# A projection stage on one core: straight code, with the next tile's norm and turn inside the tile at work

## The chip, the cores and the metric

The kernel runs on one core of one Trainium2 chip. The metric is the time of one execution on the device, in microseconds. The kernel before took 4375.03 us (median of three runs, 4374.49 to 4392.1). A profile gives one execution in detail; its times are microseconds from the first instruction.

## The reference, cut to what matters

One layer of a hybrid model in float32, for 1024 prompt rows and 8 sequences of 8 sample rows, 1024 wide. What the change touches is the first half of the layer: the norm, the projection by `w_in`, the short convolution and the mLSTM with its running state.

```
mod = silu(c) @ w_ada + b_ada                       # six rows of shift, scale and gate
h = rmsnorm(x, norm1_g) * (1 + scale1) + shift1
aq, ak, av, mqk, mv, mo, mi, mf = split(h @ w_in)   # w_in: 1024 x 3592
aq, ak = rmsnorm per head                           # k and v rows are outputs too
qk = silu(conv4(mqk)); lf = log_sigmoid(mf + b)
per chunk: b = cumsum(lf); mt = max(b + m, max(D)); wD = exp(D - mt)
           num = wg * (q @ C) + (q @ k.T * wD) @ v; den likewise with n
           hA = num / max(|den|, exp(-mt)); C, n, m = updated
hA = rmsnorm(hA) * sigmoid(mo)
att = dilated attention of aq, ak, av               # second half, not touched
x = x + gate1 * (concat(hA, att) @ w_out); x = x + gate2 * peer(...)
```

## The kernel before, in words

The program has three stages with a barrier between them. `stage0` makes the modulation rows and bias tables. `stage1`, the projection stage, makes q, k, v and the mLSTM's output. `stage3` does the attention, the output projection and the retrieval of experts, and takes most of the time; the change does not touch it.

`stage1` goes through nine tiles in order: eight of 128 prompt rows (kind "p") and one of the 64 sample rows (kind "s"). Each engine has its own list of instructions for a tile, and the lists meet by semaphores (`sig[...]`). The first tile is written out, tiles 1 to 7 are a hardware loop on each engine (`Fori`), and the sample tile is written out again. There is one buffer for x, one for the normed rows `h`, one for the turned rows `h_t`.

Within a tile the order is: ScalarE squares and sums the rows of x (L490) and makes the inverse rms (L485, L486, shared with the heads' norm); VectorE norms the rows (L665, L666); TensorE turns them by eight transposes into PSUM banks 0 and 1 (L564), and ScalarE copies them into `h_t` (L496). TensorE then multiplies `h_t` by parts of `w_in`: the gates, 8 columns wide (L569); mqk, 128 matmuls with 128 (sample tile 64) moving columns (L572); mv, mo, the two halves of qk, and av, each sixteen matmuls of 512 columns (`project`, L556). Between them stand small matmuls of the mLSTM: the cumulative sums (L579, L580), diag_a (L585), diag_m, diag_d and the selection (L588 to L590), the scores (L598), the turn of k (L601, "ktok"), the output (L613, L614), and the update of the state (L619, "cup").

VectorE's list is: gates (L668), lf (L670), the copy of mqk to `ext` and the convolution (L675 to L695), the small rows and diag_a (L698 to L702), the running maximum, diag_m and diag_d (L707 to L714), arg (L720), og (L723 to L725), scores, q_carry and kws (L729 to L742), the q and k norm (L745 to L753, ends with `qk_n`), the raw hidden rows (L759 to L765, `hraw`), their norm (L770, L771), and the state (L775 to L779). ScalarE's list is: rms, turned rows, log-sigmoid (L500 to L502), copies and exponentials of what TensorE leaves in PSUM, Silu of the convolution (L513), decay (L518), carry (L521), the squares of q and k (L528) and their inverse rms, av's copy (L534), the hidden rows' rms.

SyncE loads x for a tile as soon as the tile before has been normed (L408), then the sample rows' modulation, and after the eighth tile's state the sample's state and convolution tails (L434). GpSimd stores q, k, v and the hidden rows of each tile (L449 to L456) and, once, zeros (L462). ScalarE's queue also issues copies of the caches, 16 x 4 MB, before its first tile (L477).

Of the kernel before, what the change touches and what calls it, by code (L numbers as in the profile page):

```python
# [196 lines left out]
PER_P, PER_S = 59, 59  # L197
# [137 lines left out]
def stage1(nc, block, sig, mem, psum, const, ins, outs, scratch):  # L335
# [32 lines left out]
    s_state = work.take(DB, H_A, DK + 1)  # L368
# [36 lines left out]
    def _(sp):  # L405
# [8 lines left out]
        with sp.Fori(1, NT) as i:  # L414
            tile(i, P, ins["x"][bass.ds(i * P, P), :])
# [29 lines left out]
    def _(pool):  # L445
# [17 lines left out]
        with pool.Fori(1, NT) as i:  # L463
            store(i, P, bass.ds(i * P, P), bass.ds(i * P + WBUF - SEQ, P))
# [6 lines left out]
    def _(act):  # L471
# [8 lines left out]
        def tile(i, rows, kind, per):  # L480
            chain = Chain(act, sig["act1"], i * per)
# [6 lines left out]
            act.wait_ge(sig["x_in"], (i + 1) * 16)  # L488
            act.wait_ge(sig["h"], i)
            chain.link(nc.scalar.activation(squares[0:rows], x[0:rows], ACT.Square, accum_out=xss[0:rows]))  # L490
            inv_rms(xrs[0:rows], xln[0:rows], xss[0:rows], D, "x_rms")
            act.wait_ge(sig["h_t_ps"], i + 1)
            act.wait_ge(sig["av_ps"], i)
            for half in range(2):
                src = psum[:, half].rearrange("p (k t) -> p k t", k=4)[:, :, 0:rows]
                cp = nc.scalar.activation(h_t[:, 4 * half:4 * half + 4, 0:rows], src, ACT.Copy)  # L496
                cp.then_inc(sig["h_t"], 1)

# [3 lines left out]
            nc.scalar.activation(sm["soft"][0:rows], sm["soft"][0:rows], ACT.Ln, bias=1.0).then_inc(sig["soft"], 1)  # L502

# [9 lines left out]
            nc.scalar.activation(conv[:, :, 0:rows], conv_y[:, :, 0:rows], ACT.Silu).then_inc(sig["silu"], 1)  # L513

# [28 lines left out]
            assert chain.n == per, chain.n  # L543

        tile(0, P, "p", 7)
        with act.Fori(1, NT) as i:
            tile(i, P, "p", 7)
        tile(NT, NS, "s", 7)

    @block.tensor  # L550
    def _(pe):
        ident, ones = const["ident"], const["ones"]

        def project(bank, col, n, rows, at=0):
            for k in range(KD):
                mm = nc.tensor.matmul(psum[0:rows, bank, at:at + n], h_t[:, k, 0:rows], w_in[:, k, col:col + n], start=k == 0, stop=k == KD - 1)  # L556
            return mm

        def tile(i, rows, kind):
# [5 lines left out]
            tr.then_inc(sig["h_t_ps"], 1)  # L565
            pe.wait_ge(sig["h_t"], 2 * i + 2)
            pe.wait_ge(sig["w_in_in"], 16 * KD)
            pe.wait_ge(sig["mnew"], i)
            project(7, O_G, 2 * H_A, rows).then_inc(sig["gates_ps"], 1)  # L569
            for c in range(8):  # L570
                for k in range(KD):
                    mm = nc.tensor.matmul(psum[:, c // 4, c % 4 * P:c % 4 * P + rows], w_in[:, k, O_QK + c * P:O_QK + (c + 1) * P],  # L572
                                          h_t[:, k, 0:rows], start=k == 0, stop=k == KD - 1)
# [25 lines left out]
            mm.then_inc(sig["s_ps"], 1)  # L599
            for hh in range(H_A):  # L600
# [3 lines left out]
            project(4, 2 * W_B, W_B, rows).then_inc(sig["av_ps"], 1)  # L604
# [17 lines left out]
        tile(0, P, "p")  # L622
        with pe.Fori(1, NT) as i:
# [26 lines left out]
    def _(dve):  # L650
# [4 lines left out]
        def tile(i, rows, kind, per):  # L655
            chain = Chain(dve, sig["dve1"], dve_base + i * per)
# [6 lines left out]
            dve.wait_ge(sig["x_rms"], i + 1)  # L663
            dve.wait_ge(sig["h_t_ps"], i)
            chain.link(v.scalar_tensor_tensor(out=h[R], in0=x[R], scalar=xrs[R], in1=mod[R, 1], op0=ALU.mult, op1=ALU.mult))  # L665
            v.tensor_tensor(h[R], h[R], mod[R, 0], ALU.add).then_inc(sig["h"], 1)  # L666
# [3 lines left out]
            v.scalar_tensor_tensor(out=s("lf"), in0=gates[R, H_A:], scalar=0.0, in1=s("soft"), op0=ALU.min, op1=ALU.subtract).then_inc(sig["lf"], 1)  # L670

            dve.wait_ge(sig["mqk_ps"], i + 1)
            dve.wait_ge(sig["silu"], i)
            if kind == "p":
                chain.link(v.tensor_copy(ext_p[:, :, HALO:], psum[:, 0:2].rearrange("p a (c t) -> p (a c) t", c=4)))  # L675
# [988 lines left out]
```

## Time and profile before

| | |
|---|---|
| time, median of three runs | 4375.03 us |
| profiled execution | 4374.66 us, span 4373.0 us |
| TensorE busy over the span | 3560.7 us (81%) |
| VectorE, ScalarE, GpSimd | 2393.2, 1640.2, 1279.2 us |
| `stage1`, from the first turn to the state's store | 212.3 to 1005.4 us |
| `stage3`, from its first load | 1013.5 us to the end |

Windows give the busy time of each engine between two times, with the clock that TensorE was granted as a share of 2.4 GHz. In a timeline each row is a run of equal instructions: start, time covered, engine, line, operation, and in brackets how long the engine was idle before and which instruction ended the wait. "mem" is the on-chip memory and "psum" the accumulator banks. "PE" is TensorE, "PEld" its weight loads, "DVE" VectorE, "ACT" ScalarE, "POOL" GpSimd, "SP" SyncE. A float32 matmul is two instructions, so counts are twice those of the source.

### The profile page before, as it was taken

What the parts mean: (1) busy time and instruction counts of PE and PEld (TensorE: products, weight loads), DVE (VectorE), ACT (ScalarE), POOL (GpSimd) and SP (SyncE); (2) the same over time, 40 slices, a digit from 0 to 9 for tenths busy, and PEclk for the clock granted to TensorE, in tenths of its full rate; (3) what the DMA queues carried; (4) which work ended last, traced back from release to release, by engine and by line L of the source; (5) the groups of instructions that cost most, each with busy time, mean ns of one, the idle gap of its engine ahead of it and who ended that gap; (6) DMA issues with size and microseconds to landing.
All of it is one profiled execution on the core that took longest, in us unless ns stands there. A gap on an engine that the chain in (4) does not pass through costs nothing.

```text
span 4373.0 us, 38660 instructions
## 1 busy us (share of the span) xinstructions
PE 3560.7 (81%) x12228; PEld 1818.6 (42%) x12228; DVE 2393.2 (55%) x5587; ACT 1640.2 (38%) x4396; POOL 1279.2 (29%) x1204
## 2 busy tenths in 40 slices
PE   7288788684867987997898898789799888989877
PEld 1054454453533533443453444445345344524321
DVE  1033433322464784595486468449646845947844
ACT  0022322311335335435434533543453354334333
POOL 0000000000223343343343334234334434435433
PEclk9688888865989999999999899999999999999999
DMA  6897100146669999999999899999999999999998
GB/s 237 301 338 252 38 19 19 43 23 262 237 236 372 400 415 358 403 411 391 372 414 416 329 394 413 360 387 410 413 376 390 410 394 395 397 374 401 411 408 368
DMA packets 251979, 1419.95 MB, mean 325 GB/s; under 512 B 42963, under 2 KB 65875, under 8 KB 105603
## 3 DMA queue, kind: packets, MB, share of 16 engines
q0 software_dynamic: 168768, 1200.70, 68.4%
q1 hardware_dynamic: 79588, 132.71, 9.8%
q10 hardware_dynamic: 3440, 84.35, 5.5%
q8 instruction: 84, 1.38, 0.1%
q14 instruction: 99, 0.81, 0.1%
HBM read 1385.48 MB, written 98.73 MB: 339 GB/s over the span
## 4 chain that ended last, share of the span: by engine, by line
PE 30%; DMA 24%; DVE 11%; ACT 8%; issue 2%; POOL 0%; SPq 0%; ACTq 0%; POOLq 0%; DVEq 0%
DMA mem<-in_experts,mem 21%; PE psum L1279 20%; DVE mem L1573 6%; PE psum L1196 3%; PE psum L1178 3%; DMA mem<-key_cols 2%; ACT L1383 2%; DVE mem L1439 1%; ACT mem L1387 1%; DVE mem L1438 1%; ACT mem L1384 1%; ACT L1306 1%; PE psum L1134 1%; ACT mem L1306 1%; ACT mem L1383 1%
## 5 line engine op out<-in xcount | busy, mean ns | idle before, releaser
L1279 PE MATMUL psum<-mem 128*128 128x512 f32 (+1 forms) x4352 | 2141.1, 626 | 387.9 <-ACT mem L1387 386.4
L1104 POOL DMA_INDIRECT mem<-in_experts,mem x1088 | 1213.3, 1115 | 1872.9 <-PE psum L1279 1804.2
L1573 DVE CUSTOM_DVE_ANT_0 mem<-mem 128x1024 f32<-128x1024 f32 x1088 | 1322.8, 1222 | 708.5 <-DMA mem<-in_experts,mem 695.7
L1279 PEld LDWEIGHTS psum<-mem 128*128 128x128 f32 (+1 forms) x4352 | 776.8, 193 | 1471.1 <-ACT mem L1387 747.7
L1383 ACT ACTIVATE mem<-mem 128x1 f32<-128x1 f32 x1088 | 219.2, 201 | 1562.9 <-DVE mem L1573 1560.2
L1387 ACT ACTIVATE mem<-mem 128x128 f32<-128x128 f32 (+1 forms) x1088 | 433.3, 398 | 35.6
L556 PE MATMUL psum<-mem 128*128 128x512 f32 (+3 forms) x864 | 351.2, 558 | 10.2 <-ACT mem L496 10.2
L1384 ACT ACTIVATE mem<-mem 128x1 f32<-128x1 f32 x1088 | 320.4, 295 | 35.3
L1196 PEld LDWEIGHTS psum<-mem 128*128 128x128 f32 x2304 | 274.4, 191 | 45.2 <-issue 41.8
L1196 PE MATMUL psum<-mem 128*128 128x128 f32 (+1 forms) x2304 | 282.1, 276 | 2.5 <-ACT mem L1335 2.5
L556 PEld LDWEIGHTS psum<-mem 128*128 128x128 f32 (+1 forms) x864 | 159.7, 207 | 176.7 <-issue 162.9
L449 POOL DMA_DIRECT2D qkv_rows<-mem x9 | 5.1, 563 | 742.1 <-ACT mem L534 742.1
L564 PE MATMUL psum<-mem 128*128 128x128 f32 (+1 forms) x72 | 16.9, 415 | 192.0 <-DVE mem L666 192.0
L572 PE MATMUL psum<-mem 128*128 128x128 f32 (+1 forms) x1152 | 158.9, 310 | 0.0
L572 PEld LDWEIGHTS psum<-mem 128*128 128x128 f32 x1152 | 157.8, 226 | 0.0
L1416 DVE CUSTOM_DVE_ANT_0 mem<-psum,mem 128x128 f32<-128x128 f32 (+7 forms) x64 | 48.4, 756 | 192.7 <-PE psum L1136 166.0
L1438 DVE MAX8 mem<-mem 128x8 f32<-128x128 f32 (+3 forms) x432 | 145.8, 338 | 12.5
L1439 DVE FIND_INDEX8 mem<-mem 128x8 uint32<-128x128 f32 (+3 forms) x432 | 141.9, 328 | 0.0
L1178 PE MATMUL psum<-mem 128*128 128x512 f32 (+1 forms) x288 | 135.5, 595 | 0.0
L1134 PE MATMUL psum<-mem 64*128 64x512 f32 (+3 forms) x160 | 67.9, 531 | 56.3 <-DMA mem<-key_cols 56.2
L303 PE MATMUL psum<-mem 128*9 128x512 f32 x192 | 91.7, 637 | 20.0 <-DMA mem<-in_b_ada 13.9
L1383 ACT ACT_TABLE_LOAD x80 | 102.6, 1283 | 14.0 <-DVE mem L1573 12.6
(255 smaller groups left out, 2612.4 us busy)
## 6 DMA issues: line engine op xcount, KB each, us to landing
out_k_s<-in_cache_k ACTq DMA_DIRECT2D x8, 4080.0 KB, 125.1
out_v_s<-in_cache_v ACTq DMA_DIRECT2D x8, 4080.0 KB, 137.4
mem<-in_w_ada SPq DMA_DIRECT2D x12, 2048.0 KB
mem<-mod_rows SPq DMA_DIRECT2D x34, 512.0 KB
mem<-in_experts,mem POOLq DMA_INDIRECT x1088, 9.7
mem<-in_keys_t POOLq DMA_DIRECT2D x16, 1024.0 KB, 6.8
mem<-in_vals POOLq DMA_DIRECT2D x16, 1024.0 KB, 8.4
mem<-in_w_in ACTq DMA_DIRECT2D x8, 1796.0 KB, 24.8
```

What stands on the lines that cost most here:

```text
L556: mm = nc.tensor.matmul(psum[0:rows, bank, at:at + n], h_t[:, k, 0:rows], w_in[:, k, col:col + n], start=k == 0, stop=k == KD - 1)
L572: mm = nc.tensor.matmul(psum[:, c // 4, c % 4 * P:c % 4 * P + rows], w_in[:, k, O_QK + c * P:O_QK + (c + 1) * P], h_t[:, k, 0:rows], start ...
L1104: pool.indirect_dma_start(out=ring[:, g % N_SLOTS].rearrange("p a n -> p (a n)"), out_offset=None, in_=ins["experts"][:, :], in_offset=bas ...
L1178: mm = nc.tensor.matmul(psum[0:r, out_banks(n)[half]], turned[:, k, 0:r], w_out[:, k, half * 512:(half + 1) * 512], start=k == 0, stop=k = ...
L1196: mm = nc.tensor.matmul(psum[:, 5, j % 4 * P:j % 4 * P + r], w_q[:, k, j * NKEY:(j + 1) * NKEY], turned[:, k, 0:r], start=k == 0, stop=k = ...
L1279: mm = nc.tensor.matmul(psum[0:r, half], diag[:, g % 4, 0:r], ring[:, g % N_SLOTS, 1, half * 512:(half + 1) * 512], start=c == 0, stop=c = ...
L1383: chain.link(a.activation(act_v[:, c:c + 1], dots[:, c:c + 1], ACT.Gelu))
L1384: chain.link(a.activation(weight[:, c:c + 1], act_v[:, c:c + 1], ACT.Copy, scale=gate[i % 2][:, c:c + 1]))
L1387: a.activation(diag[:, g % 4, 0:r], spread, ACT.Copy, scale=weight[:, c:c + 1]).then_inc(sig["diag"], 1)
L1438: chain.link(v.max(values[:, e:e + 8], src))
L1439: chain.step(v.max_index(places[:, e:e + 8], values[:, e:e + 8], src))
L1573: v.tensor_tensor_reduce(row, row, h2[i % 2], 1.0, 0.0, ALU.mult, ALU.add, dots[:, c:c + 1]).then_inc(sig["dots"], 1)
```

## The change

- The hardware loops on all engines become straight code, so that waits compare with constants.
- The norm and turn of a tile become functions (`rows_rms`, `turned` on ScalarE, `turn` on TensorE, `normed` on VectorE). They are called for tile 0 ahead of the tiles, and for tile i + 1 inside tile i: the rms after the log-sigmoid, the norm after lf, the turn after mo, the copies after Silu.
- A second buffer for the turned rows lies in the room of the sample rows' state, which is loaded after the eighth tile; tiles take turns (`h_ts[i % 2]`).
- On TensorE mv moves ahead of mqk, the first half of qk ahead of diag_a's matmul, the second half between diag_a's and diag_m's. The wait for `hraw` and `kws` of the tile before stands ahead of mqk, that for arg ahead of ktok. diag_a's matmul goes to bank 4, diag_m's to bank 1.
- On VectorE the small rows and diag_a move ahead of the convolution.
- The sample tile's wait for the convolution tails stays at the head of its tile, which now begins with the gates.

The diff, cut: what is moved unchanged is not shown again, nor the loops of SyncE and GpSimd, which change in the same way, nor the bank numbers on VectorE.

```diff
@@ -365,7 +364,9 @@
-    s_state = work.take(DB, H_A, DK + 1)
+    s_room = work.take(DB * H_A * (DK + 1))
+    s_state = s_room.rearrange("p (b h e) -> p b h e", b=DB, h=H_A)
+    h_ts = (h_t, s_room[:, 0:KD * P].rearrange("p (k t) -> p k t", k=KD))
@@ -477,29 +478,40 @@
+        def rows_rms(i, rows):
+            act.wait_ge(sig["x_in"], (i + 1) * 16)
+            act.wait_ge(sig["h"], i)
+            if i >= 2:
+                act.wait_ge(sig["qss"], i - 1)
...
+        def turned(i, rows):
+            act.wait_ge(sig["h_t_ps"], i + 1)
+            if i >= 2:
+                act.wait_ge(sig["av_ps"], i - 1)
...
             nc.scalar.activation(sm["soft"][0:rows], sm["soft"][0:rows], ACT.Ln, bias=1.0).then_inc(sig["soft"], 1)
+            if i < NT:
+                rows_rms(i + 1, P if i + 1 < NT else NS)
...
             nc.scalar.activation(conv[:, :, 0:rows], conv_y[:, :, 0:rows], ACT.Silu).then_inc(sig["silu"], 1)
+            if i < NT:
+                turned(i + 1, P if i + 1 < NT else NS)
@@ -540,68 +554,83 @@
-        tile(0, P, "p", 7)
-        with act.Fori(1, NT) as i:
-            tile(i, P, "p", 7)
-        tile(NT, NS, "s", 7)
+        rows_rms(0, P)
+        turned(0, P)
+        for i in range(NT):
+            tile(i, P, "p")
+        tile(NT, NS, "s")
...
+        def turn(i, rows):
             pe.wait_ge(sig["h"], i + 1)
-            pe.wait_ge(sig["hraw"], i)
-            pe.wait_ge(sig["kws"], i)
+            if i >= 1:
+                pe.wait_ge(sig["ext"], i)
...
+        def tile(i, rows, kind):
             pe.wait_ge(sig["h_t"], 2 * i + 2)
...
+            project(i, 7, O_G, 2 * H_A, rows).then_inc(sig["gates_ps"], 1)
+            if i >= 1:
+                pe.wait_ge(sig["scores"], i)
+            project(i, 5, O_MV, W_A, rows).then_inc(sig["mv_ps"], 1)
+            if i >= 1:
+                pe.wait_ge(sig["hraw"], i)
+                pe.wait_ge(sig["kws"], i)
...
-            pe.wait_ge(sig["scores"], i)
-            project(5, O_MV, W_A, rows).then_inc(sig["mv_ps"], 1)
...
-            project(6, O_MO, W_A, rows).then_inc(sig["mo_ps"], 1)
+            project(i, 6, O_MO, W_A, rows).then_inc(sig["mo_ps"], 1)
+            if i < NT:
+                turn(i + 1, P if i + 1 < NT else NS)
+            if i >= 1:
+                pe.wait_ge(sig["state"], i)
+            project(i, 2, 0, W_B, rows)
 
             pe.wait_ge(sig["diag_a"], i + 1)
-            pe.wait_ge(sig["state"], i)
-            nc.tensor.matmul(psum[0:rows, 2, 0:H_A * rows], ones[0:rows, 0:rows], diag_a_of(rows), start=True, stop=True).then_inc(sig["a_rep"], 1)
+            if i >= 1:
+                pe.wait_ge(sig["av"], i)
+            nc.tensor.matmul(psum[0:rows, 4, 0:H_A * rows], ones[0:rows, 0:rows], diag_a_of(rows), start=True, stop=True).then_inc(sig["a_rep"], 1)
+            project(i, 3, W_B, W_B, rows).then_inc(sig["qk_ps"], 1)
             pe.wait_ge(sig["diag_m"], i + 1)
-            pe.wait_ge(sig["av"], i)
-            nc.tensor.matmul(psum[0:rows, 3, 0:H_A * rows], ones[0:rows, 0:rows], diag_m_of(rows), start=True, stop=True)
+            if i < NT:
+                pe.wait_ge(sig["h_t"], 2 * i + 4)
+            nc.tensor.matmul(psum[0:rows, 1, 0:H_A * rows], ones[0:rows, 0:rows], diag_m_of(rows), start=True, stop=True)
...
-            project(2, 0, W_B, rows)
-            pe.wait_ge(sig["arg"], i + 1)
-            project(3, W_B, W_B, rows).then_inc(sig["qk_ps"], 1)
             pe.wait_ge(sig["silu"], i + 1)
...
             mm.then_inc(sig["s_ps"], 1)
+            pe.wait_ge(sig["arg"], i + 1)
...
             pe.wait_ge(sig["carry"], i + 1)
-            project(4, 2 * W_B, W_B, rows).then_inc(sig["av_ps"], 1)
+            project(i, 4, 2 * W_B, W_B, rows).then_inc(sig["av_ps"], 1)
@@ -652,31 +681,48 @@
+        def normed(i, rows):
+            R = slice(0, rows)
+            dve.wait_ge(sig["x_rms"], i + 1)
+            if i >= 1:
+                dve.wait_ge(sig["h_t_ps"], i)
...
             v.scalar_tensor_tensor(out=s("lf"), in0=gates[R, H_A:], scalar=0.0, in1=s("soft"), op0=ALU.min, op1=ALU.subtract).then_inc(sig["lf"], 1)
+            if i + 1 < NT:
+                normed(i + 1, P)
+            if i + 1 == NT:
+                dve.wait_ge(sig["mod_in"], 64)
+                normed(NT, NS)
...
+                v.tensor_copy(ext_p[:, :, HALO:], psum[:, 0:2].rearrange("p a (c t) -> p (a c) t", c=4)).then_inc(sig["ext"], 1)
+                dve.wait_ge(sig["ext"], i + 1)
...
+            dve.wait_ge(sig["b_ps"], i + 1)
+            chain.step(v.tensor_copy(s("b"), psum[R, 7, 8:12]))
...
@@ -777,22 +816,19 @@
-        tile(0, P, "p", PER_P)
-        with dve.Fori(1, NT) as i:
-            tile(i, P, "p", PER_P)
-        dve.wait_ge(sig["mod_in"], 64)
+        normed(0, P)
+        for i in range(NT):
+            tile(i, P, "p")
         dve.wait_ge(sig["s_conv_in"], 16 * 8)
...
+        tile(NT, NS, "s")
```

## Rows read from the trace of the kernel before

**Rows 1.** Windows by tile: start:end, length, busy by engine, TensorE clock, DMA share

```profile
294.39:376.54 82.15, 65.28 (x280) 42.78 (x280) 32.47 (x76) 24.21 (x43) 2.16 (x4) 0.85 1.01 344
...
458.44:540.30 81.86, 65.21 (x280) 42.69 (x280) 32.47 (x76) 24.21 (x43) 2.15 (x4) 0.85 0.07 26
212.29:294.39 82.10, 65.50 (x280) 42.86 (x281) 32.45 (x76) 24.20 (x43) 4.72 (x6) 0.85 0.99 333
```

**Rows 2.** Timeline, TensorE, eighth tile: start us, length us, idle before in brackets

```profile
786.10 1.97 PE L564 MATMUL psum<-mem 128*128 128x128 f32 x8 [12.10 <-DVE mem L666]
...
789.25 3.58 PE L556 MATMUL psum<-mem 128*128 128x8 f32 x16 [1.18 <-ACT mem L496]
...
792.68 16.39 PE L572 MATMUL psum<-mem 128*128 128x128 f32 x128
...
827.55 2.07 PE L588 MATMUL psum<-mem 128*128 128x512 f32 x2 [3.42 <-DVE mem L714]
...
831.07 13.98 PE L556 MATMUL psum<-mem 128*128 128x512 f32 x32
...
853.09 0.38 PE L613 MATMUL psum<-mem 128*128 128x129 f32 x2
...
854.87 1.06 PE L619 MATMUL psum<-mem 128*128 128x129 f32 x8
```

**Rows 3.** Timeline, VectorE and ScalarE, eighth tile

```profile
795.06 0.16 DVE L670 SCALAR_TENSOR_TENSOR mem<-mem 128x4 f32<-128x4 f32 x1 [2.03 <-ACT mem L502]
...
831.64 0.69 DVE L720 TENSOR_TENSOR mem<-mem,psum 128x512 f32<-128x512 f32 x1
...
833.55 0.57 ACT L521 ACTIVATE mem<-psum 128x512 f32<-128x512 f32 x1
...
836.09 0.69 DVE L725 TENSOR_TENSOR mem<-mem 128x512 f32<-128x512 f32 x1
...
846.05 0.69 DVE L729 TENSOR_TENSOR mem<-psum,mem 128x512 f32<-128x512 f32 x1 [9.27 <-PE psum L598]
...
852.32 1.23 DVE L753 TENSOR_TENSOR mem<-mem 128x1024 f32<-128x1024 f32 x1
...
863.87 0.42 DVE L779 TENSOR_TENSOR mem<-mem,psum 128x258 f32<-128x258 f32 x1
```

**Rows 4.** Windows with the granted clock: mqk of the fourth tile; sample tile

```profile
467.00:468.90 1.90, 1.90 (x11) 1.90 (x10) 0.50 0.00 0
468.90:471.00 2.10, 2.10 (x21) 2.10 (x21) 1.00 0.00 0
...
935.00:940.00 5.00, 2.69 (x10) 1.00 (x9) 2.78 (x12) 3.67 (x4) 0.00 (x0) 0.99 1.79 4
940.00:945.00 5.00, 5.00 (x9) 1.47 (x8) 4.40 (x4) 1.52 (x7) 0.00 (x0) 0.66 1.03 4
```

**Rows 5.** DMA issues, early tiles: count, KB, us to landing

```profile
mem<-in_x SPq DMA_DIRECT2D x1, 512.0 KB, 27.8
...
out_v_p<-mem POOLq DMA_DIRECT2D x1, 256.0 KB, 55.6
mix_rows<-mem POOLq DMA_DIRECT2D x1, 256.0 KB, 62.7
...
out_v_p<-mem POOLq DMA_DIRECT2D x1, 256.0 KB, 47.2
```

**Rows 6.** Timeline, sample tile

```profile
884.28 1.28 DVE L665 SCALAR_TENSOR_TENSOR mem<-mem 64x1024 f32<-64x1024 f32 x1 [19.98 <-DMA mem<-in_conv_tail]
...
886.87 1.11 PE L564 MATMUL psum<-mem 64*128 64x64 f32 x8 [30.94 <-DVE mem L666]
...
890.54 27.57 PE L572 MATMUL psum<-mem 128*128 128x64 f32 x128
...
937.73 0.64 PE L588 MATMUL psum<-mem 64*64 64x256 f32 x2 [2.31 <-DVE mem L714]
...
963.49 10.43 PE L630 MATMUL psum<-mem 128*128 128x8 f32 x64 [0.68 <-ACT mem L534]
```

More of the change, by code:

```diff
@@ L413, in _ @@
         tile(0, P, ins["x"][0:P, :])
-        with sp.Fori(1, NT) as i:
-            tile(i, P, ins["x"][bass.ds(i * P, P), :])
+        for i in range(1, NT):
+            tile(i, P, ins["x"][i * P:(i + 1) * P, :])
         sp.wait_ge(sig["h"], NT)
@@ L462, in _ @@
             pool.dma_start(outs[name][0:WBUF - SEQ].rearrange("(p r) (a n) -> p (r a) n", p=P, a=2), bc(zeros, 1, 2 * (WBUF - SEQ) // P)).then_inc(sig["zeros_out"], 16)
-        with pool.Fori(1, NT) as i:
-            store(i, P, bass.ds(i * P, P), bass.ds(i * P + WBUF - SEQ, P))
+        for i in range(1, NT):
+            store(i, P, slice(i * P, (i + 1) * P), slice(WBUF - SEQ + i * P, WBUF - SEQ + (i + 1) * P))
         store(NT, NS, slice(SEQ, NTOK))
@@ L478, in _ @@
         lnscale, eps = const["lnscale"], const["eps"]
-        def tile(i, rows, kind, per):
-            chain = Chain(act, sig["act1"], i * per)
+        chain = Chain(act, sig["act1"])
+        def rows_rms(i, rows):
[3 more added lines that the diff above has]
+                act.wait_ge(sig["qss"], i - 1)
+            chain.link(nc.scalar.activation(squares[0:rows], x[0:rows], ACT.Square, accum_out=xss[0:rows]))
+            chain.link(nc.scalar.activation(xln[0:rows], xss[0:rows], ACT.Ln, scale=1.0 / D, bias=eps[0:rows]))
+            nc.scalar.activation(xrs[0:rows], xln[0:rows], ACT.Exp, scale=-0.5).then_inc(sig["x_rms"], 1)
+        def turned(i, rows):
+            act.wait_ge(sig["h_t_ps"], i + 1)
+            if i >= 2:
+                act.wait_ge(sig["av_ps"], i - 1)
+            for half in range(2):
+                src = psum[:, half].rearrange("p (k t) -> p k t", k=4)[:, :, 0:rows]
+                cp = nc.scalar.activation(h_ts[i % 2][:, 4 * half:4 * half + 4, 0:rows], src, ACT.Copy)
+                cp.then_inc(sig["h_t"], 1)
+        def tile(i, rows, kind):
             def inv_rms(out, tmp, total, n, event):
@@ L486, in inv_rms @@
                 nc.scalar.activation(out, tmp, ACT.Exp, scale=-0.5).then_inc(sig[event], 1)
[L488 to L497, printed above, removed]
             act.wait_ge(sig["gates"], i + 1)
@@ L620, in tile @@
                 mm.then_inc(sig["cup"], 1)
-        tile(0, P, "p")
-        with pe.Fori(1, NT) as i:
+        turn(0, P)
+        for i in range(NT):
             tile(i, P, "p")
@@ L653, in _, with tile @@
         taps = const["conv"]
-        def tile(i, rows, kind, per):
-            chain = Chain(dve, sig["dve1"], dve_base + i * per)
+        def normed(i, rows):
[3 more added lines that the diff above has]
+                dve.wait_ge(sig["h_t_ps"], i)
+            chain.link(v.scalar_tensor_tensor(out=h[R], in0=x[R], scalar=xrs[R], in1=mod[R, 1], op0=ALU.mult, op1=ALU.mult))
+            v.tensor_tensor(h[R], h[R], mod[R, 0], ALU.add).then_inc(sig["h"], 1)
+        def tile(i, rows, kind):
             R = slice(0, rows)
@@ L679, in tile @@
                 dve.wait_ge(sig["s_ext"], 8)
+            dve.wait_ge(sig["b_ps"], i + 1)
+            chain.step(v.tensor_copy(s("b"), psum[R, 7, 8:12]))
+            chain.step(v.tensor_copy(s("blast"), psum[R, 7, 12:16]))
+            chain.link(v.tensor_tensor(s("a"), gates[R, 0:H_A], psum[R, 7, 8:12], ALU.subtract))
+            chain.step(v.tensor_scalar(s("a_s"), s("a"), lnscale[R], None, ALU.add))
+            v.tensor_tensor(heads_of(diag_a, rows), bc(ident[R, R], 1, H_A), bc(s("a"), 2, rows), ALU.mult).then_inc(sig["diag_a"], 1)
             for j in range(CONV_W):
@@ L695, in tile @@
                 v.tensor_copy(ext_p[:, :, 0:HALO], ext_p[:, :, P:P + HALO]).then_inc(sig["halo"], 1)
-            dve.wait_ge(sig["b_ps"], i + 1)
-            chain.step(v.tensor_copy(s("b"), psum[R, 7, 8:12]))
-            chain.step(v.tensor_copy(s("blast"), psum[R, 7, 12:16]))
-            chain.link(v.tensor_tensor(s("a"), gates[R, 0:H_A], psum[R, 7, 8:12], ALU.subtract))
-            chain.step(v.tensor_scalar(s("a_s"), s("a"), lnscale[R], None, ALU.add))
-            v.tensor_tensor(heads_of(diag_a, rows), bc(ident[R, R], 1, H_A), bc(s("a"), 2, rows), ALU.mult).then_inc(sig["diag_a"], 1)
             dve.wait_ge(sig["a_rep"], i + 1)
@@ L706, in tile @@
                 dve.wait_ge(sig["s_state_in"], 32)
-            chain.link(v.tensor_tensor(arg_of(rows), heads_ps(2, rows, rows), bc(const[kind + "_neg"][R], 1, H_A), ALU.add))
+            chain.link(v.tensor_tensor(arg_of(rows), heads_ps(4, rows, rows), bc(const[kind + "_neg"][R], 1, H_A), ALU.add))
             chain.link(v.tensor_reduce(s("cmax"), arg_of(rows), AX.X, ALU.max))
@@ L785, in _ @@
         v.memset(sm["mprev"], 0.0).then_inc(sig["dve1"], 1)
[L786 to L787 removed]
+        dve.wait_ge(sig["dve1"], 4)
         dve.wait_ge(sig["mod_in"], 32)
[L789 to L792 removed]
+        chain = Chain(dve, sig["dve1"], 4)
+        normed(0, P)
+        for i in range(NT):
+            tile(i, P, "p")
         dve.wait_ge(sig["s_conv_in"], 16 * 8)
[L794 to L795 removed]
+        tile(NT, NS, "s")
         chain = Chain(dve, sig["s_state_steps"])
```

29 lines of the change are left out of this document (9 added, 20 removed).

## The prediction

> **What bounds the kernel now.** I read the windows first, one for each tile of the projection stage: it is nine tiles long, and a prompt tile takes 81.9 to 82.15 us, in which TensorE is busy for 65.2, VectorE for 32.5 and ScalarE for 24.2 [rows 1]. TensorE is the longest engine, but 16.7 us of every tile it does nothing, so no engine bounds the stage by itself. The timeline of one tile says where [rows 2]: 12.10 us before the eight transposes at L564, which wait for the next tile's norm on VectorE, 1.18 us before the gates' matmuls (ScalarE copies the turned rows out of PSUM), and 3.42 us at L588 (VectorE makes diag_m). The 12.10 us are one chain: TensorE ends at 855.93 with L619 [rows 2], VectorE ends the state at 864.29 [rows 3], ScalarE's rms and VectorE's norm follow. The first two tiles run while old copies fill the DMA engines (DMA share 0.99 and 1.01, against 0.07 later), and take no longer for it [rows 1].
>
> The idle time costs twice. After it TensorE's clock is granted at 0.50 (1.2 GHz) until 468.9 in the tile that starts at 458.44 and at 1.00 (2.4 GHz) from there [rows 1, 4]. Of these 10.46 us, 1.18 are idle, so the work in them would take 4.6 us less at 2.4 GHz. At L588 four 512-column matmuls and a small one take from 827.55 to 831.07, 3.52 us, where sixteen take 6.99 [rows 2]: another 1.6 us. TensorE's work at full clock is thus 65.2 - 4.6 - 1.6 = 59.0 us a tile.
>
> **A steady prompt tile after the change.** Time 0 is the end of the tile before's L619. The next tile's transposes and their copies now stand inside this tile, so its first matmuls wait for nothing: the 12.10 and 1.18 us go. The 3.42 us go too, since a projection of 6.99 us now stands between diag_a's matmul and diag_m's, and VectorE needs 3.4 us in that place. What is late next, engine by engine:
> - VectorE ends the old tile's state at 8.36 (864.29 - 855.93). Then come the gates and lf, 2.5 us (from 792.68, the end of the gates' matmuls, to 795.22) [rows 2, 3], at about 11. TensorE wants lf only after gates, mv (6.99) and mqk (13.8, half of the 27.57 that 128 such pieces take at 1.2 GHz [rows 6]), at 22.5: hidden, 11 us to spare. The moved rms and norm follow; in the old tile both lay in the 12.10 us, so they end by 23, and the ext copy follows mqk at 24; the turn starts at 29.5: hidden. The two copies of the turned rows come after Silu, near 36, and are wanted at 45: hidden.
> - The added wait on arg, ahead of ktok: after the m matmuls VectorE needs until 832.33 for arg, 1.25 us past 831.07 [rows 2, 3]; the scores' matmuls cover 0.9. Stall 0.4.
> - carry was covered by two projections; now only ktok (0.45) stands before the av projection that waits for it, and carry ends 1.8 us after arg (834.12 - 832.33) [rows 3]. Stall 1.35.
> - The last matmuls (L619) wait for qk_n. From arg VectorE needs 4.45 us for og (836.78 - 832.33) and then, from scores to the last qk product, 7.5 us (846.05 to 853.55) [rows 3], in all 11.95. TensorE needs 0.45 + 1.35 + 6.99 + 1.78 (854.87 - 853.09 [rows 2]) = 10.6. Stall 1.35.
>
> The sum is 59.0 + 3.1 = 62.1 us a tile if the clock stays at 2.4 GHz. It will not quite: from the last stall over L619 to the gates' 8-column matmuls lie four sparse microseconds. The trace has no such stretch; the nearest row is the sample tile's, where a wait of 2.31 us among small matmuls was followed by a mean clock of 0.66 over 5 us, a loss of (1 - 0.66) x 5 = 1.7 us [rows 4, 6]. Bounds are 0 (nothing falls) and 5.4: gates at half rate (1.8), then 4 us of projection at half rate (2.0) as in the old tile's start, and the old L588's 1.6 again at carry. I take 1.7, the nearest row: 63.8 us. From the second tile's start (294.39) to the eighth's (786.10) the old tiles took 491.71, 81.95 each [rows 1, 2]; 7 x (81.95 - 63.8) = 127.0 us gained.
>
> On the clock the Trainium skill ("TensorE: Matmul & The Clock Gate", section "HAM oscillation — how this bites in real kernels") puts the fall down to long idle gaps between bursts of matmuls. By that alone stalls of 1.35 us would leave 2.4 GHz and the tile would take 62.1, a rival below; the row with 2.31 us speaks against it.
>
> **The first tiles, under the copies.** ScalarE's and VectorE's queues now hold the next tile's rms and norm in the middle, and behind them the whole conv and mlstm work, so the load of x must have landed. The second tile's x is asked for at 212.4, as the first turn starts [rows 1], and takes 27.8 us [rows 5]: 240.6 with its issue, norm done at 246.3, 4.6 after mqk. TensorE is at mo until 249 then; ext is copied at 247.5 and the turn waits for nothing. The first tile's L619 ends at 280.8 instead of 282.3 (294.39 less a wait of 12.1 [rows 1, 2]): 1.5 gained. Later loads are asked for a whole tile ahead. Had this one taken the 62.7 us of the slowest row [rows 5], 33 us would be lost once.
> Stores come closer. The first tile's v rows were on their way 55.6 us, its mix rows 62.7 [rows 5]; in the second tile qkv is wanted at 341 (landed at 337), and the old hid at 344 (landed at 351): what waits is the hraw chain, whose 7 us TensorE's gates and mv cover. The second tile's v rows, issued near 344, land between 391 (47.2 us [rows 5]) and 411.7, when the old ones did with the same bytes to drain; they are wanted at 404 ahead of qk_n, on the path. 0 to 8 us; I take the middle, 4 lost. SP's loop becomes straight code that waits for the same norms; POOL's stores keep their order.
>
> **The sample tile.** Its norm waited with the rest for the conv tails (19.98 us, TensorE idle for 30.94 [rows 6]). That wait now stands ahead of its gates' add only; norm and turn lie in the eighth tile, and gates, mv and mqk run at once. lf comes 28.35 + 2.5 = 30.85 after L619 (884.28 - 855.93 [rows 6]). mqk starts at 9 and ends at 23 (full clock) to 37 (half: in the old run these 64-column pieces never left 1.2 GHz though TensorE had no pause). I take 34, since mv's wide columns start it fast. From mqk's end to L630 the old run took 45.4 us (918.1 to 963.49 [rows 6]), 9.4 of it mv, which is now ahead: 36.0. L630 starts at 70 instead of 107.56: 37.5 gained, bounds 34.5 and 40.8. All behind it stays, and the third stage does not touch what moves.
>
> **Sum.** 127.0 + 1.5 - 4 + 37.5 = 162.0. The profiled execution took 4374.66 (span 4373.0 and 1.66 around it), 0.4 under the median of 4375.03, so the forecast is 4213 us.
>
> **Rivals.**
> - The clock stays up and the stores are in time: 62.1 a tile, 12 us less, and the 4 back: 4197. For it: no stall above 1.4 us. Against: the 2.31 us row [rows 6].
> - The clock falls in both sparse stretches: bound 5.4 in place of 1.7, 3.7 x 7 = 26 more: 4239. For it: the old tile's slow start.
> - The unrolling itself gains or costs. Straight code (first tile, 82.10), a loop's first pass (82.15) and a later one (81.86) [rows 1] differ by 0.3 us at most, so a back edge is worth 2 us in seven tiles unless the 12.10 us hid it; if it hid a price, that goes with the wait. The other way, new code for each tile must come in while copies fill the DMA engines; at the price of a load there (27.8) in the three tiles under them: 4213 + 83 = 4296. That is also the case in which the change does not do what it says, since the overlap is lost while engines stand.
> - Slower than before: a denser stage does not hold 2.4 GHz. mqk in the sample tile is the row that speaks for it: 27.57 us at 1.2 GHz without a pause [rows 6]. At 1.2 GHz throughout a tile takes 2 x 59.0 + 3.1 = 121.1 us, 39.2 more than 81.95, in all 274 lost against some 36 gained elsewhere: about 4613. It decides from 23 us lost a tile (162 / 7), which is 46 us of each tile spent at half clock. Against it: within the old tile, 128-column matmuls bring the clock up to 1.00 [rows 4], and with the five projections they are 48.8 of the 59.0 us.
>
> **How the numbers follow.** Chances: the forecast 0.45 (4203 to 4225), full clock 0.22, two falls 0.22, code or loads late in the first tiles 0.07, half clock 0.03, no effect 0.01. 0.5% is 22 us, about what a measurement of this kernel tells from no change. Only the last two cases are not faster by that: faster 0.96, same 0.01, slower 0.03. The range takes in both clock cases, the bounds of the sample tile and a few us either way for the third stage: 4183 to 4250.
>
> **What would show it.** Right: about 64 us between two L619 groups, no idle over 2 us on TensorE inside a prompt tile, waits for arg, carry and qk_n of 0.4 to 1.4 us, the clock mostly at 1.00, L630 about 70 us after the eighth L619. Wrong: a wait at the turn for the ext copy or the norm, VectorE reaching qk_n later than 12 us after arg, a tile longer than 68 us, the sample tile's mqk waiting for anything, or a third stage of another length.

## The result and the profile after

The changed kernel takes 4200.59 us (median of four runs, 4191.22 to 4221.66) against 4380.3 us for the kernel before (median of four): a ratio of 0.959 (95% interval 0.955 to 0.964). Forecast were 4213 us and a range of 4183 to 4250. The profiled execution took 4200.74 us, its span 4199.0, 174.0 under the span of before.

Where the 174.0 us came from, read off the starts of the same groups of matmuls in the two timelines of TensorE (a cup's end is taken 1.00 us behind its start, here and in every run below):

| part | before | after | difference | forecast |
|---|---|---|---|---|
| start to the first turn | 212.29 | 203.89 | -8.4 | 0 |
| first turn to the first cup | 69.04 | 67.61 | -1.4 | -1.5 |
| first cup to the eighth (seven tiles) | 573.54 | 450.63 | -122.9 | -123.0 |
| eighth cup's end to the sample's state matmuls | 107.6 | 66.0 | -41.6 | -37.5 |
| from there to the end | 3409.5 | 3409.8 | +0.3 | 0 |

The first and the last row belong to code that the change does not touch. In the profiles of the ten runs below the first turn stands between 204.2 and 208.8, and the part behind the sample's state matmuls takes 3401 to 3428 us, so 20 us between the spans of two single runs say nothing here. The lengths of tiles, most of which repeat to 0.05 us, do.

The windows by tile of the kernel after (start:end, length, busy by engine, TensorE clock, DMA share, GB/s), from the second tile to the sample tile, cut at the end of cup (L648), where those of before were cut at the turn [rows 1]:

```profile
272.47:334.20 61.73, 59.27 (x282) 37.95 (x281) 31.23 (x71) 21.19 (x41) 4.74 (x7) 1.00 0.99 341
334.20:405.64 71.44, 59.54 (x278) 37.87 (x277) 33.19 (x82) 21.31 (x41) 2.15 (x5) 0.95 0.91 324
405.64:472.82 67.18, 64.71 (x286) 41.51 (x285) 32.21 (x77) 21.30 (x41) 2.15 (x5) 0.92 0.09 32
472.82:537.92 65.10, 62.63 (x282) 39.67 (x281) 32.20 (x77) 21.19 (x41) 2.15 (x5) 0.95 0.09 33
537.92:599.65 61.73, 59.27 (x282) 37.95 (x281) 32.20 (x77) 21.19 (x41) 2.14 (x5) 1.00 0.09 35
...
723.09:789.17 66.08, 55.92 (x250) 28.47 (x248) 23.03 (x78) 17.81 (x35) 1.34 (x3) 0.92 0.90 64
```

Four of the seven tiles take 61.7 us at a clock of 1.00, with 59.27 us of work where the prediction had 59.0. Three are longer, and in these the clock is below 1.00: 71.44, 67.18 and 65.10.

A regular tile in TensorE's timeline of the kernel after, the sixth. It answers to the 12.10, 1.18 and 3.42 us of before [rows 2]: the turn (L579), the gates (L570, x32 with mv) and diag_m (L614) wait for nothing. What is left are 0.18 us for arg (L630), 1.13 for carry (L570) and 1.15 for qk_n (L648).

```profile
537.92 8.82 PE L570 MATMUL psum<-mem 128*128 128x8 f32 x32
546.58 14.45 PE L597 MATMUL psum<-mem 128*128 128x128 f32 x128
...
568.18 1.04 PE L579 MATMUL psum<-mem 128*128 128x128 f32 x8
...
575.93 1.02 PE L614 MATMUL psum<-mem 128*128 128x512 f32 x2
...
586.83 0.66 PE L630 MATMUL psum<-mem 128*128 128x128 f32 x4 [0.18 <-DVE mem L759]
588.62 7.13 PE L570 MATMUL psum<-mem 128*128 128x512 f32 x16 [1.13 <-ACT mem L535]
...
598.69 1.13 PE L648 MATMUL psum<-mem 128*128 128x129 f32 x8 [1.15 <-DVE mem L792]
```

The same timeline at the long tiles. The third tile's last matmuls wait 10.28 us for qk_n (L792). After that wait cup takes 2.06 us instead of 1.13, gates and mv 13.37 instead of 8.82. A tile later gates and mv take 12.18 us with no wait longer than 1.15 us since.

```profile
404.68 2.06 PE L648 MATMUL psum<-mem 128*128 128x129 f32 x8 [10.28 <-DVE mem L792]
406.53 13.37 PE L570 MATMUL psum<-mem 128*128 128x8 f32 x32
...
471.86 1.13 PE L648 MATMUL psum<-mem 128*128 128x129 f32 x8 [1.15 <-DVE mem L792]
472.82 12.18 PE L570 MATMUL psum<-mem 128*128 128x8 f32 x32
```

The waits in the stage (engine, what waited <- what it waited for: total us, times, longest) say why: VectorE's L789, on the way to qk_n, stands behind a store of v rows, the second tile's, before it may write over them.

```profile
DVE mem L701 <- DMA mem<-in_conv_tail: 20.0, 1, 20.0
...
DVE mem L789 <- DMA out_v_p<-mem: 11.0, 1, 11.0
```

GpSimd issued that store at 334.46, and VectorE could go on at 402.05:

```profile
334.46 0.54 POOL L453 DMA_DIRECT2D out_v_p<-mem  x1
...
402.05 1.23 DVE L789 TENSOR_TENSOR mem<-psum,mem 128x1024 f32<-128x1024 f32 x1 [11.04 <-DMA out_v_p<-mem]
```

The granted clock behind the two cups, the third tile's and the fourth's (windows; the clock is the third column from the end): 0.50 after the long wait, 0.66 and then 0.50 behind the later cup.

```profile
406.50:410.00 3.50, 3.50 (x19) 3.50 (x18) 0.00 (x0) 3.45 (x10) 0.00 (x0) 0.50 0.82 305
...
472.80:476.00 3.20, 3.20 (x19) 2.83 (x18) 0.45 (x2) 2.69 (x10) 0.81 (x2) 0.66 0.91 347
476.00:480.00 4.00, 4.00 (x6) 1.69 (x5) 2.21 (x4) 1.66 (x3) 0.54 (x1) 0.50 0.14 54
```

The sample tile after, which answers to the 30.94 us wait and the 27.57 us of mqk [rows 6]: mqk (L597) starts at once and runs in 14.51 us. Then TensorE waits 7.75 us for lf, which waits for the conv tails (20.0 us, above). The state matmuls start 66.0 us after the eighth cup's end, at 723.1.

```profile
723.19 8.02 PE L570 MATMUL psum<-mem 128*64 128x8 f32 x32
731.14 14.51 PE L597 MATMUL psum<-mem 128*128 128x64 f32 x128
753.40 0.37 PE L602 MATMUL psum<-mem 64*64 64x4 f32 x2 [7.75 <-DVE mem L703]
...
789.17 11.92 PE L659 MATMUL psum<-mem 128*128 128x8 f32 x64 [1.40 <-ACT mem L548]
```

### The profile page after: what moved, and what is told of

The parts are those of the page before. It is cut to its first block, busy times and chain, and to the rows that moved or that the text cites. A ratio compares the mean times of both kernels' runs of the same rounds, so it can differ in the third digit from the quotient of the medians.

```text
span 4199.0 us, 38253 instructions
## 1 busy us (share of the span) xinstructions
PE 3506.4 (84%) x12228; PEld 1773.9 (42%) x12228; DVE 2390.4 (57%) x5587; ACT 1615.9 (38%) x4380; POOL 1274.8 (30%) x1204
## 4 chain that ended last, share of the span: by engine, by line
PE 31%; DMA 26%; DVE 11%; ACT 8%; issue 2%; POOL 0%; SPq 0%; ACTq 0%; POOLq 0%; DVEq 0%
DMA mem<-in_experts,mem 22%; PE psum L1315 20%; DVE mem L1609 6%; PE psum L1232 3%; PE psum L1214 3%; DMA mem<-key_cols 3%; ACT L1419 1%; DVE mem L1475 1%; ACT mem L1423 1%; DVE mem L1474 1%; ACT mem L1420 1%; PE psum L1170 1%; ACT L1342 1%; ACT mem L1419 1%; ACT mem L1342 1%
## 5 line engine op out<-in xcount | busy, mean ns | idle before, releaser
L1315 PEld LDWEIGHTS psum<-mem 128*128 128x128 f32 (+1 forms) x4352 | 773.3, 192 | 1463.1 <-ACT mem L1423 746.7
L570 PE MATMUL psum<-mem 128*128 128x512 f32 (+3 forms) x864 | 346.5, 553 | 11.0 <-ACT mem L535 9.8
L1232 PEld LDWEIGHTS psum<-mem 128*128 128x128 f32 x2304 | 274.4, 191 | 45.1 <-issue 41.7
L1232 PE MATMUL psum<-mem 128*128 128x128 f32 (+1 forms) x2304 | 282.1, 276 | 2.5 <-ACT mem L1371 2.5
L570 PEld LDWEIGHTS psum<-mem 128*128 128x128 f32 (+1 forms) x864 | 151.4, 194 | 179.7 <-issue 165.9
L597 PEld LDWEIGHTS psum<-mem 128*128 128x128 f32 x1152 | 129.9, 192 | 5.3 <-issue 4.2
L597 PE MATMUL psum<-mem 128*128 128x128 f32 (+1 forms) x1152 | 130.2, 274 | 0.3 <-DVE mem L804 0.3
L1609 DVE DVE_READ_ACCUMULATOR2_ANT mem<- 128x1 f32 x1088 | 89.8, 83 | 0.0
```

What stands on the lines that cost most here:

```text
L570: mm = nc.tensor.matmul(psum[0:rows, bank, at:at + n], h_ts[i % 2][:, k, 0:rows], w_in[:, k, col:col + n], start=k == 0, stop=k == KD - 1)
L1232: mm = nc.tensor.matmul(psum[:, 5, j % 4 * P:j % 4 * P + r], w_q[:, k, j * NKEY:(j + 1) * NKEY], turned[:, k, 0:r], start=k == 0, stop=k = ...
L1315: mm = nc.tensor.matmul(psum[0:r, half], diag[:, g % 4, 0:r], ring[:, g % N_SLOTS, 1, half * 512:(half + 1) * 512], start=c == 0, stop=c = ...
L1609: v.tensor_tensor_reduce(row, row, h2[i % 2], 1.0, 0.0, ALU.mult, ALU.add, dots[:, c:c + 1]).then_inc(sig["dots"], 1)
```

## The experiments

Each edit is to the changed kernel, except the first. "Seven tiles" is the stretch from the first cup to the eighth (450.63 us in the changed kernel), "sample" the one from the eighth cup's end to the sample's state matmuls (66.0). Straight code, the four moves together and the last run have medians of several executions; the seven edits between were executed once each, under the profiler, so what counts of them are these lengths and not their times.

**Straight code alone.** The kernel before, its loops over tiles 1 to 7 written out.

```diff
-        with pe.Fori(1, NT) as i:
+        for i in range(1, NT):          # on all five engines
```

> The kernel before with its hardware loops written out as straight code, nothing else changed. Theory A (the gain is the overlap, and straight code is worth nothing by itself): a prompt tile stays at 81.9 us, from the first L619's end to the eighth's 573 us within 3, the time within 0.5% of before. Rival B (branches cost something that the 12.1 us wait hid, or that lay on the path): tiles 2 to 8 are at least 2 us shorter each, 14 us or more in all, and TensorE's wait before its turn falls below 11 us. Rival C (new code must come in while the copies run): the second and third tile become longer than 84 us.

4376.49 us against 4382.19, ratio 0.9985 (0.9964 to 1.0007). Seven tiles take 573.65 us (before 573.54), under the copies as without them. In the old order straight code is worth nothing and costs nothing; the gain is in the order of the work. The Trainium skill ("Runtime: NRT & Kernel Launch", section "Instruction fetch mechanics") lets a taken branch whose target is not at hand cost a fetch of it. By these 0.1 us no such cost shows in seven passes of this loop.

**The sample tile's norm and turn behind the eighth tile again.** The rest of the new order is kept.

```diff
-            if i < NT:
-                turn(i + 1, P if i + 1 < NT else NS)
+            if i < NT - 1:
+                turn(i + 1, P)          # and so for rms, norm and copies
...
+        turn(NT, NS)
```

> The changed kernel, but the sample rows are normed and turned at the head of their own tile, behind the wait for the convolution tails, as before. Theory A (the sample tile gains because its wide and narrow projections no longer stand behind that wait): from the eighth L619's end to the sample tile's first 8-column state matmul it takes 105 us within 4 again in place of 66.1, and mqk's 64-column matmuls take 27 us again in place of 14.5, since TensorE comes out of a wait of 30 us at 1.2 GHz; the prompt tiles keep 61.7 us. Time about 39 us over the changed kernel's, near 4240. Rival B (mv ahead of mqk is what made the sample tile short): it stays below 80 us.

The sample takes 91.55 us, between the two expectations. Its timeline:

```profile
746.84 1.09 PE L581 MATMUL psum<-mem 64*128 64x64 f32 x8 [30.20 <-DVE mem L696]
748.68 11.03 PE L572 MATMUL psum<-mem 128*64 128x8 f32 x32 [0.75 <-ACT mem L500]
759.63 14.51 PE L599 MATMUL psum<-mem 128*128 128x64 f32 x128
```

The wait for the conv tails is back (30.20 us), and yet mqk takes 14.51 us. So 25.5 of the 41.6 us gained come from working through that wait, and the other 16.1 from the new order within the tile: with mv's wide columns ahead of it mqk alone is 13.1 us faster than the 27.57 of before [rows 6]. The remaining 3 were not traced to one cause.

**The zeros later.** The two 2 MB stores of zeros on GpSimd's queue go from behind the first tile's stores to behind the fifth's.

```diff
-        pool.wait_ge(sig["zeros"], 1)   # and the two stores of zeros
         for i in range(1, NT):
             store(i, ...)
+            if i == 4:
+                pool.wait_ge(sig["zeros"], 1)   # and the two stores
```

> The changed kernel with the two 2 MB stores of zeros issued behind the fifth tile's stores in place of the first's. Theory A (the third tile's wait of 10.28 us before L648 is its predecessor's v rows queued behind the zeros while the caches are copied): those rows land within 56 us of their issue as the first tile's did before, that is by 391, and the wait falls to the 1.15 us of the other tiles; the half clock behind it goes too, so 9 us and 4.5 us more are gained in the third and fourth tile, and the eight prompt tiles end 12 to 15 us earlier. Rival B (the copies alone hold the stores): the wait stays above 6 us.

All seven tiles take 61.70 to 61.75 us, 432.12 in all: 18.5 less than in the changed kernel, and 12.9 less than the 444.99 of its second profile (last experiment); expected were 12 to 15. No fall of the clock is left; cup waits 1.2 us at most.

```profile
337.80:399.50 61.70, 59.27 (x280) 37.96 (x280) 32.24 (x78) 21.18 (x41) 2.14 (x4) 1.00 0.83 295
399.50:461.30 61.80, 59.27 (x280) 37.95 (x280) 32.27 (x78) 21.19 (x41) 2.13 (x4) 1.00 0.09 35
```

The long wait for the v rows' store needs the zeros, and the slow fourth tile behind it went with it: 71.44 and 67.18 less 2 x 61.73 are 15.2 of the 18.5 us. The other 3.4 are the fall in the fifth tile, which is missing as well from five profiles that keep the zeros and the long wait (the second of the changed kernel, the sample late, og, both, the conv tails); it is not shown to be the zeros' doing. That the stage began 3.9 us later in this profile is not the reason: in the last experiment below the changed kernel begins later still, at 208.83, and waits 9.16 us.

**Both halves of qk behind diag_m, not ahead.** Only the diag_a matmul, which stood between the halves, stays ahead of diag_m.

```diff
-            project(i, 2, 0, W_B, rows)     # and the wait for state ahead of it
             # diag_a's matmul stands here
-            project(i, 3, W_B, W_B, rows).then_inc(sig["qk_ps"], 1)
             # diag_m, diag_d and the selection stand here
+            project(i, 2, 0, W_B, rows)
+            project(i, 3, W_B, W_B, rows).then_inc(sig["qk_ps"], 1)
```

> The changed kernel with TensorE's two halves of qk back behind the matmuls of diag_m, as before; the norm and turn stay inside the tile at work. Theory A (moving qk covers VectorE's making of diag_m): TensorE waits 5 to 6 us before diag_m's matmul in each prompt tile (that matmul must also wait for VectorE's convolution, which now ends later than the turn), the waits before ktok, av and L648 vanish because qk covers them again, and a tile takes 64 to 66.5 us in place of 61.7: 16 to 33 us more over the seven tiles. Rival B (the order does not matter, whatever is not waited for there is waited for at L648): 61.7 us within 0.7.

Tiles of 66.0 to 67.4 us in turn, some of them longer than the 64 to 66.5 expected; 467.12 in all, 16.5 more than in the changed kernel and 35.0 more than with the zeros later, which is the fairer measure, since here too no tile is slowed by a store. The waits for arg, carry and qk_n are gone; one wait of 5.65 us has come, and diag_m runs at half clock behind it (2.08 us, in the changed kernel 1.02):

```profile
519.25 2.08 PE L614 MATMUL psum<-mem 128*128 128x512 f32 x2 [5.65 <-DVE mem L752]
```

Of these 5.65 us VectorE is at the end of its convolution for the first 2.3 (diag_a's matmul ends at 513.60, the running maximum starts at 515.87) and at the running maximum and diag_m for the other 3.3. So the second half, between diag_a and diag_m, does cover VectorE's running maximum, as the prediction said, and the first half covers the convolution; the two are worth some 5 us a tile.

**og's arithmetic ahead of the wait for the m matmuls.** VectorE does it (a reciprocal of 3.35 us among it) right behind diag_d, where it stood idle for these matmuls (5.37 us in the third tile), and not after arg.

```diff
             # running maximum, diag_m, diag_d
+            dve.wait_ge(sig["og"], i + 1)   # og + 1, reciprocal, gain: up
             dve.wait_ge(sig["m_rep"], i + 1)
             # the small rows, arg
-            dve.wait_ge(sig["og"], i + 1)   # from here
```

> The changed kernel with VectorE's three operations on og (4.45 us) moved from behind arg to ahead of its wait for the m matmuls, where it stands idle for some 5.5 us a tile. Theory A (two paths lead from arg to the last matmuls: TensorE's own, 10.5 us, and VectorE's to qk_n, 11.95 us): TensorE's wait of 1.15 us before L648 goes, the others (0.18 before ktok, 1.13 before av) stay, a tile takes 60.4 to 60.7 us in place of 61.73. Rival B (qk_n is held by ScalarE's inverse rms or by the qk projection, not by og): 61.7 us and the same wait.

The wait before cup is gone, the one for carry stays; tiles of 60.31 to 60.36 us, 1.4 less, a little under the expectation. The third tile's v rows are still late (9.51 us, 72.33).

**carry ahead of the four decay exponentials on ScalarE, and of the wait for arg.**

```diff
+            act.wait_ge(sig["m_rep"], i + 1)        # and the wait for state
+            nc.scalar.activation(carry..., ACT.Exp)
             # the waits for arg and scores, decay
-            nc.scalar.activation(carry..., ACT.Exp)
```

> The changed kernel with ScalarE's carry exponential ahead of the four decay exponentials and without waiting for arg, which it doesn't read. Theory A: TensorE's wait before av goes from 1.13 us to nothing, and comes back before L648, which still waits for qk_n 11.95 us after arg: 2.2 to 2.4 us there in place of 1.15, and a tile takes 61.7 us as before. Rival B (the path through TensorE sets the end): a tile takes 60.6 us.

The waits came nearly as expected: none for carry, 2.55 us before cup (4.06 in the third tile, whose store is late). The tiles did not: 65.03 to 65.10 us from the fifth on, 66.6 to 66.7 before. The timeline shows a thing that neither theory had:

```profile
472.59 1.13 PE L649 MATMUL psum<-mem 128*128 128x129 f32 x8 [2.55 <-DVE mem L793]
473.56 12.18 PE L571 MATMUL psum<-mem 128*128 128x8 f32 x32
```

and the windows behind that cup its clock:

```profile
472.60:475.60 3.00, 3.00 (x22) 3.00 (x23) 1.26 (x5) 1.57 (x9) 1.60 (x3) 0.80 0.61 235
475.60:480.00 4.40, 4.40 (x8) 2.31 (x9) 1.52 (x3) 2.78 (x4) 0.00 (x0) 0.50 0.37 142
```

Gates and mv take 12.18 us instead of 8.82: two waits of 1.13 and 1.15 us with 9 us of work between them leave the clock up in the changed kernel's regular tiles; after one of 2.55 it falls in every tile, which costs 3.36 us more here and at least 3.3 in each of the others.

**Both.**

> Both at once: og ahead of the wait for the m matmuls, carry ahead of decay. Theory A: both waits go, a tile takes 59.3 to 59.7 us in place of 61.73 (2.3 us less: 1.15 and 1.13), of TensorE's waits only the 0.18 us before ktok is left, and the seven tiles are 16 us shorter where no store is late. Rival B: the time saved at one place comes back at another wait and a tile stays above 60.5 us.

Tiles of 58.91 to 58.96 us, a little under the expectation, with 0.18 us of waits: nothing but work. Together the two moves are worth 2.8 us a tile, where the second alone cost 3.3. But the third tile waits 12.26 us for its store.

**The conv tails ahead of the state's store on SyncE's queue.** The store of the conv rows, which they wait for, moves with them.

```diff
+        sp.wait_ge(sig["halo"], NT)         # the conv rows' store, its wait, the eight conv tails
         sp.wait_ge(sig["state"], NT)        # and the two stores, the state's load
-        sp.wait_ge(sig["halo"], NT)         # from here, and the wait with the tails
```

> The changed kernel in which SyncE stores the prompt's convolution rows and loads the sample's convolution tails when the eighth tile's convolution is done, ahead of its wait for the eighth tile's state. Theory A (the sample tile is now bound by those tails: gates' add 28.35 us after the eighth L619, then lf, for which TensorE waits 7.75 us behind mqk): the wait before the cumulative sums goes, and so does the half clock behind it; from the eighth L619's end to the first 8-column state matmul it takes 56 to 58.5 us in place of 66.1. Rival B (the state's load and its chain end later anyway): above 63 us.

The sample takes 56.42 us, 9.6 less, and the 7.75 us wait is gone, so lf, by way of the conv tails, was what bounded it. (Unedited the same code takes 66.0, 67.4 and 68.0 us in three profiles.)

**The four moves together, and the changed kernel once more.**

> The four moves together: the zeros of k_p and v_p stored after the fifth tile, og's arithmetic ahead of qk_n, carry ahead of the scores' copy, and the sample's conv tails loaded ahead of the state's store. Theory A (each wait has one cause and they are independent): seven prompt tiles of 58.95 us as e7 had them without the store wait, 412.7 in all against 450.6 in the changed kernel; no wait of TensorE above 0.4 us inside a prompt tile; the sample tile 56.4 us as in e8. Against the changed kernel 37.9 + 9.6 + 2.7 in the first tile = 50 us less, a span of about 4149 us. Theory B (the zeros, put off, meet the stores of faster tiles again, or the loads of the conv tails are late behind them): a wait of some us before the last matmuls of the sixth or seventh tile, with half clock behind it, or the sample tile above 60; a span of 4160 or more.

> The changed kernel itself, once more. Theory A (the fall of the clock in the fifth tile, with no wait above 1.2 us ahead of it, is left over from the two slow tiles before it): the third tile waits about 10 us for the v rows again, the fourth and the fifth tiles are again 67 and 65 us long, the other four 61.7. Theory B (the fall in the fifth tile comes by chance after any wait of 1.15 us): the tile with a fall is another one, or there is none, or more than one. The span 4190 to 4205 either way.

On one chip: 4170.26 us for the four, ratio to before 0.952 (0.949 to 0.954), and 4212.19 for the changed kernel, 0.961 (0.959 to 0.964). In their profiles, in the order of the table above: -1.7 before the stage, -3.1 in the first tile, -21.7 in the seven tiles (423.29 against 444.99), -13.1 in the sample (54.83 against 67.97), +0.8 behind it. The new version is the fastest that was run, 42 us under the changed kernel, but its seven tiles are 10.6 us short of Theory A, and something like Theory B is there, in the third tile though, not in the sixth or seventh. Its timeline in the third tile:

```profile
331.76 8.82 PE L572 MATMUL psum<-mem 128*128 128x8 f32 x32
343.38 16.19 PE L599 MATMUL psum<-mem 128*128 128x128 f32 x128 [2.80 <-DVE mem L806]
...
397.04 1.13 PE L650 MATMUL psum<-mem 128*128 128x129 f32 x8 [2.35 <-DVE mem L794]
398.00 12.15 PE L572 MATMUL psum<-mem 128*128 128x8 f32 x32
```

and the waits from 330 to 420 us:

```profile
DVE mem L800 <- DMA mix_rows<-mem: 11.1, 1, 11.1
...
DVE mem L791 <- DMA out_v_p<-mem: 4.7, 1, 4.7
```

The zeros do not stand ahead of these stores now. The shorter tiles bring the third one to the stores of the first tile's hidden rows and of the second's v rows before these have landed, and each wait has slow matmuls behind it (mqk 16.19 us for 14.45, gates and mv 12.15 for 8.82). The third and fourth tiles take 66.23 and 62.35 us, the five others 58.9. This run and the one with both moves issue the second tile's v rows at the same point, 124.8 and 124.7 us after the first turn; VectorE has them free 187.3 us after it here, and 196.9 after it with the zeros ahead of them. So the zeros are worth 9.6 us of that store, and the rest of its time is not theirs.

The changed kernel's second profile has 70.11 and 66.24 us in the third and fourth tiles (a wait of 9.16 for the v rows), as the first had, but 61.74 in the fifth. So the long wait and the slow tile behind it recur; the fall in the fifth does not (nor did it with the sample late, og, both or the conv tails moved). Theory A has the first right and is wrong on the fifth. A fall of this kind shows once more, in the eighth tile of the kernel with the sample late, four tiles behind its last long wait (the clock is 0.58 from 656 to 660 us):

```profile
652.95 1.13 PE L650 MATMUL psum<-mem 128*128 128x129 f32 x8 [1.15 <-DVE mem L794]
653.92 10.52 PE L572 MATMUL psum<-mem 128*128 128x8 f32 x32
```

In the five profiles with both short waits (the changed kernel twice, the sample late, the zeros later, the conv tails) 35 tiles start behind a wait of 1.15 us, and two of them have a fall. That is nearer to Theory B. What decides it stays open.

## Why the prediction was right, step by step

- **What goes.** The 12.10, 1.18 and 3.42 us went, the last for the reason given (the qk experiment). VectorE's and ScalarE's moved work is hidden; neither norm nor turn is ever late.
- **What is late next.** The three new waits stand where they were forecast, at 0.18, 1.13 and 1.15 us against 0.4, 1.35 and 1.35. The og and carry experiments show the causes of the last two, and that they are tied: whoever takes away only the carry wait finds all of it, and more, before cup. Work and waits make 61.73, forecast 62.1.
- **The clock, mis-sized.** The 1.7 us added to every tile were wrong: in four tiles it is 0, and in seven the forecast had 12 us too many. The row taken, a wait of 2.31 us [rows 4, 6], holds for such a wait (one of 2.55 us cost 3.36, twice the 1.7), not for two of 1.13 and 1.15. The rule that the prediction weighed, long idle gaps, is the Trainium skill's ("TensorE: Matmul & The Clock Gate", section "HAM oscillation — how this bites in real kernels"). It agrees with the four tiles that kept the clock, with all seven when the zeros are later, and with the falls behind the long waits (7.16 to 12.26 us). It has no place for the fifth tile's fall, or for those behind 2.55 us.
- **The stores, mis-sized.** Forecast 4 us, the middle of bounds of 0 and 8. The third tile lost 9.7 (9.1 of them the wait, 10.28 in place of 1.15) and the fourth 5.5 to the clock behind it. By the prediction's own signs this is a case of being wrong: a tile over 68 us, a wait over 2, qk_n 21 us after arg. Three steps failed. Of its two times for the v rows the later one, when the old ones landed with the same bytes to drain, was right, 199.4 us after the first turn (411.7 less 212.29) against a measured 198.2 (402.05 less 203.89); the middle was taken. VectorE wanted to write at 187.1 (391.01 less 203.89), not at 191.7 (404 less 212.29), mostly because two tiles of 61.73 had run and not two of 63.8. And no price was put on the clock after that wait.
- **The errors cancel.** Seven tiles were forecast at 7 x 63.8 + 4 = 450.6 and took 450.63, from 7 x 61.73, 15.2 for the store and 3.4 for the fall in the fifth tile. The errors are not independent, since a clock that stays up makes the wait longer; but that they meet to 0.1 us is luck. The second profile of the same kernel has 444.99. With the tiles at 61.73 and the 4 as they were the sum would have been 14.5 us too low; with 18.5 and the tiles as they were, 14.5 too high.
- **The sample tile.** lf came 30.2 us after the eighth cup's end (forecast 30.85). mqk ended at 22.5, not at the chosen 34 but by the other bound, 23, since the clock stayed up. So TensorE waited for lf, and 66.0 came out in place of 70. This term was mis-sized by 4.1 us: the wrong one of its two bounds for mqk was near the one taken.
- **Rivals.** Straight code at no price, as the first experiment shows. "Half clock throughout" was as wrong as a case can be. The rival with the clock up, 4197, was nearer to the median in us, but half of its condition (stores in time) failed; with the zeros put off it holds, in one execution of 4190.73 us.
- **The rest** of the 12 us between the forecast and the profiled execution is the 8.4 before the stage and 4.1 in the sample tile. No edit here varied the code ahead of the stage; its length scatters by 5 us between the ten runs, and the old order in straight code has 206.1 there, so the 8.4 are not shown to be the change's.

## What to carry to other kernels

When work is moved to close a long wait, list the stores that the shorter loop will catch up with, and price each wait that is left over with the clock that falls behind it: here 10.28 us of waiting cost 15.2 in the tile that waited and the next. Split or shorten leftover waits before moving one: two of 1.13 and 1.15 us were 3.3 us cheaper a tile than one of 2.55, and removing both paid where removing one lost. And compare terms, not sums: this forecast's seven tiles were right to 0.1 us out of two errors of 14.5 us each.

## What the runs showed of the hardware

- The sample tile's mqk (64 moving columns) kept the level of the clock that it started with in all twelve profiles: 27.57 us at 0.50 before [rows 6], 14.51 at 1.00 after, also behind a wait of 30.20 us when gates and mv (11.03 us) ran in between.
- While the copies of the caches (queue q10) run, GpSimd's queue (q0) moves as many packets as they do and a small part of the bytes: 366 packets each from 320 to 380 us of the kernel after, 18.67 MB against 1.37. When the copies are through, near 390, it moves 3.52 MB in 15 us. The two queues from 320 to 380 us, then the second from 395 to 410 (packets, MB, share of the 16 DMA engines):

```profile
q10 hardware_dynamic: 366, 18.67, 91.8%
q0 software_dynamic: 366, 1.37, 5.6%
...
q0 software_dynamic: 858, 3.52, 58.9%
```

- So the time at which a store here is done hangs less on its issue than on what stands ahead of it when the copies end. In seven profiles with the 4 MB of zeros ahead of the second tile's 256 KB of v rows VectorE had these free 194.6 to 198.2 us after the first turn, though they were issued anywhere from 124.7 to 135.1 us after it. With the zeros put off it was 187.3 in the kernel of the four moves, and 189.2 at the latest with the zeros alone put off, when VectorE went on without a wait for them.
